# The second feed-forward part by seven block products, in two phases of 768 tokens

## What is computed

```
x += 0.5 * g1 * swiglu(modulate(rmsnorm(x), sh1, sc1), ffn1)
x += g2 * concat(window_attention, mla_attention) @ w_out
x += 0.5 * g3 * swiglu(modulate(rmsnorm(x), sh3, sc3), ffn2)
x  = rmsnorm(x)

def swiglu(h, wg, wu, wd):          # wg, wu: 1024 x 2816, wd: 2816 x 1024
    return (silu(h @ wg) * (h @ wu)) @ wd
```

## Time and profile before

| | |
|---|---|
| median of three runs | 3179.14 us |
| profiled execution, its own span | 3173.7 us |
| TensorE busy in it | 3075.7 us, 97% |
| VectorE, ScalarE, GpSimd busy | 1526.7, 956.5, 802.9 us |
| first matmul of the out-projection | 1928.30 us |
| matmuls in the span | 14129 |

### The profile page before, as it was taken

How to read it: one execution, slowest core, us unless ns; L and a number is a source line. 1 busy time by engine, 2 the same in 40 slices (tenths; PEclk the granted TensorE clock), 3 DMA queues, 4 the chain that set the end, 5 groups by cost and what they waited for, 6 DMA issues and landing times.

```text
span 3173.7 us, 40407 instructions
## 1 busy us (share of the span) xinstructions
PE 3075.7 (97%) x14129; PEld 2457.0 (77%) x14129; DVE 1526.7 (48%) x2651; ACT 956.5 (30%) x1669; POOL 802.9 (25%) x531
## 2 busy tenths in 40 slices
PE   7999999999999989997989999999999999999998
PEld 3888888888888868885656667788888888888887
DVE  5576667776671266886544331542322123231234
ACT  6311111111111146766767774331111111111112
POOL 0111111111111143334557665421111111111110
PEclk9999999999999999998999999999999999999999
DMA  7121212212121023557322244211110110101102
GB/s 267 39 69 57 62 52 79 68 58 64 48 74 34 27 95 124 144 146 168 99 59 75 78 105 130 84 43 34 33 33 26 40 32 27 33 26 40 33 27 87
DMA packets 282857, 223.60 MB, mean 70 GB/s; under 512 B 17179, under 2 KB 254094, under 8 KB 282766
## 3 DMA queue, kind: packets, MB, share of 16 engines
q1 hardware_dynamic: 282766, 222.41, 23.8%
...
## 4 chain that ended last, share of the span: by engine, by line
PE 43%; POOL 8%; issue 6%; DVE 3%; ACT 1%; SPq 1%; DMA 0%; DVEq 0%; POOLq 0%; ACTq 0%
PE PS L479 14%; PE PS L480 13%; PE PS L481 13%; POOL XT_r L1956 8%; PE PS L735 0%; PE PS L1655 0%; DVE XT L648 0%; DVE PS L634 0%; ACT z_sb L1173 0%; DVE y_sb L2221 0%; PE PS L1692 0%; DVE kT_st L1358 0%; SPq L2003 0%; DMA scr_kb<-kT_st 0%; ACT hid_hi L578 0%
## 5 line engine op out<-in xcount | busy, mean ns | idle before, releaser
L479 PE MATMUL PS<-H_hi,W_hi 128*128 128x512 f32 x2304 | 900.6, 391 | 1.4 <-DVE H_lo L1910 1.4
L480 PE MATMUL PS<-H_lo,W_hi 128*128 128x512 f32 x2304 | 897.0, 389 | 0.0
L481 PE MATMUL PS<-H_hi,W_lo 128*128 128x512 f32 x2304 | 896.9, 389 | 0.0
L473 POOL TENSOR_TENSOR W_lo<-raw,W_hi 128x1024 fp32r<-128x1024 f32 x132 | 317.2, 2409 | 1846.8 <-ACT W_hi L441 1846.8
L648 DVE SCALAR_TENSOR_TENSOR XT<-PS,mod,XT 128x512 f32<-128x512 f32 x528 | 395.1, 749 | 301.7 <-PE PS L481 301.5
L479 PEld LDWEIGHTS PS<-H_hi,W_hi 128*128 128x128 f32 x2304 | 432.9, 188 | 94.1 <-issue 2.5
L441 ACT ACTIVATE W_hi<-raw 128x1024 fp32r<-128x1024 f32 x132 | 137.3, 1056 | 1215.5 <-PE PS L481 1214.4
L480 PEld LDWEIGHTS PS<-H_lo,W_hi 128*128 128x128 f32 x2304 | 432.9, 188 | 90.6 <-issue 1.4
L481 PEld LDWEIGHTS PS<-H_hi,W_lo 128*128 128x128 f32 x2304 | 432.8, 188 | 89.8
L634 DVE TENSOR_TENSOR PS<-hid_g,PS 128x512 f32<-128x512 f32 x132 | 91.6, 694 | 763.2 <-PE PS L481 753.1
L479 PE MATMUL PS<-hid_hi,W_hi 128*128 128x512 f32 x1056 | 417.1, 395 | 4.2 <-DVE XT L648 2.7
...
## 6 DMA issues: line engine op xcount, KB each, us to landing
...
raw<-in_ffn_wg SPq DMA_DIRECT2D x44, 512.0 KB, 4.0
raw<-in_ffn_wu SPq DMA_DIRECT2D x44, 512.0 KB, 4.0
raw<-in_ffn_wd SPq DMA_DIRECT2D x44, 512.0 KB, 3.6
...
raw<-in_w_out SPq DMA_DIRECT2D x22, 512.0 KB, 3.6
...
```

What stands on the lines that cost most here:

```text
L473: pool.tensor_tensor(W_lo[:, n % WS, :], raw[:, n % RS, :], W_hi[:, n % WS, :].bitcast(F32), ALU.subtract).then_inc(w_ready, 1)
L479: pe.matmul(out, w_hi, m_hi, start=first, stop=False)
L480: pe.matmul(out, w_hi, m_lo, start=False, stop=False)
L481: return pe.matmul(out, w_lo, m_hi, start=False, stop=last)
```

## The change

The second feed-forward part is written anew, and the out-projection before it is cut in four chunks of 384 tokens in place of three of 512.

The block scheme: the 1024 input features are two halves, the 256 hidden columns of a round are two halves, and the 768 tokens of a phase are two halves of 384. Gate (or up) of a round is then a product of 2x2 blocks with 2x2 blocks, eight block products in the plain form. Here it is seven, with sums of weight blocks (A11, A12, A21 + A22 and so on, 7 weight units a round, gate in the left and up in the right half of a unit) and sums of activation blocks (B11, B21, T1 to T4, B22). A block product has 4 blocks of features by 3 matmuls, for gate and for up. Results are collected in four pairs of PSUM banks: ScalarE keeps copies of some (`part_keep_act`), VectorE adds them back (`st_add_dve`). Down stays plain: 16 steps of 6 matmuls with 384 columns, in eight banks in turn.

There are 22 rounds: phase 0 takes tokens 0 to 767 through 11 rounds, phase 1 the tokens 768 to 1535, so each weight is read and split twice. Weights come in quarters of 128x4x128 for gate and up (`quart`, four pairs a round), GpSimd makes the four weight sums (`st_sum`) and nine low splits a round. The activation operands of a phase are built once: `op_x_dve` normalises a block of 768 columns, `op_shift_act` adds the shift, `op_t_dve` makes a difference T of 4x384 columns, `op_hi_act` copies high, `op_lo_dve` makes the low part. For phase 0 that happens during the last chunk of the out-projection and behind it, for phase 1 in round 10 and the beginning of round 11.

The diff, cut to its core:

```
+NB = 384
+HT = 2 * NB
+NR = FT // 2
+NWC = TOK // NB
+UN = 9
+PN = 7
+B11, B21, T1, T2, T3, T4, B22 = range(PN)
...
         def wo_act(act):
-            for i in range(NCH * KD):
+            for i in range(NWC * KD):
                 if i >= RS:
                     wo_split_hi(act, i)
                 c, m = i // KD, i % KD
...
+                if c == NWC - 1:
+                    if m < 4:
+                        op_shift_act(act, 0, 2 * m)
+                        op_shift_act(act, 0, 2 * m + 1)
+                    else:
+                        for j in ((B11, B21), (T1,), (T2,), ())[m - 4]:
+                            op_hi_act(act, 0, j)
+            for j in (T3, T4, B22):
+                op_hi_act(act, 0, j)
...
         def wo_dve(dve):
-            for i in range(NCH * KD):
+            for i in range(NWC * KD):
...
+                gate_add(dve, i % WOB, 1, m, c, wo_added)
+                if c == NWC - 1:
+                    if m < 2:
+                        op_x_dve(dve, 0, 2 * m)
+                        op_x_dve(dve, 0, 2 * m + 1)
+                    elif m == 2:
+                        op_t_dve(dve, 0, T1)
+                        op_x_dve(dve, 0, 4)
+                        op_x_dve(dve, 0, 5)
...
+        def op_x_dve(dve, h, k):
+            if h == 0 and k == 0:
+                dve.wait_ge(wo_done, (NWC - 1) * KD)
+                dve.wait_ge(rstd_ready, 2 * NCH + 2)
+            if h == 1 and k == 0:
+                dve.wait_ge(st_steps, st_at(NR - 1, product_step(T3, 1)))
+                dve.wait_ge(rstd_ready, 2 * NCH + NWC)
+            if h == 1 and k == KD // 2:
+                dve.wait_ge(st_steps, st_at(NR - 1, product_step(B22, 1)))
+            row = SLf[:, KD * (k // 4) + 4 + k % 4, 0:2, :].rearrange("p c n -> p (c n)")
+            by = (rstd_a, rstd_b)[h][:, :, :].rearrange("p c n -> p (c n)")
+            for a, b, s, a0, b0 in phase_span(h):
+                mm = dve.scalar_tensor_tensor(out=row[:, a0:b0], in0=XT[:, k, a:b], scalar=hscale[:, 2, k, s:s + 1],
+                                              in1=by[:, a0:b0], op0=ALU.mult, op1=ALU.mult)
+            mm.then_inc(op_x, 1)
+        def op_shift_act(act, h, k):
+            act.wait_ge(op_x, OPX0 + h * XN + (k + 1 if k < KD // 2 else k + 2))
+            row = SLf[:, KD * (k // 4) + 4 + k % 4, 0:2, :].rearrange("p c n -> p (c n)")
+            for _, _, s, a0, b0 in phase_span(h):
+                mm = act.activation(row[:, a0:b0], row[:, a0:b0], ACT.Identity, bias=mod[:, SH3 * KD + k, s:s + 1])
+            mm.then_inc(op_shift, 1)
+        OP_T = {T1: (T3, B11), T2: (B22, T1), T4: (B21, T2), T3: (B22, T3)}
...
+        UNIT_FROM = (A11Q, A12Q, None, A11Q, A21Q, A22Q, A12Q)
...
+        def st_hi_act(act, R, u, nxt=0):
+            if u in (0, 1, 5):
+                act.wait_ge(quart_landed[UNIT_FROM[u]], R * 32 + (32 * nxt + 32 + QUART0))
+            elif u < PN:
+                act.wait_ge(sum_ready, R * 4 + (4 * nxt + {2: 1, 3: 3, 4: 2, 6: 4}[u]))
+            else:
+                act.wait_ge(down_landed[u - PN], R * 16 + (16 + DOWN0))
+            if is_round(R, 0) and u < 3 and not nxt:
+                act.wait_ge(wo_done, NWC * KD - 2 + u)
+            elif u < 3:
+                act.wait_ge(st_steps, st_at(R, SN * nxt - SN + (2 * PN if u == 0 else SN)))
+            else:
+                act.wait_ge(st_steps, st_at(R, 2 * (u - 3) + 2))
+            act.activation(W_hi[:, st_slot(u), :], unit_src(u), ACT.Copy).then_inc(unit_hi, 1)
...
+        def st_sum(pool, R, no, nxt=0):
+            out, a, b, op = ((qsum[:, :, :], quart[:, A21Q], quart[:, A22Q], ALU.add),
+                             (quart[:, A21Q], quart[:, A11Q], quart[:, A21Q], ALU.subtract),
+                             (quart[:, A11Q], qsum[:, :, :], quart[:, A11Q], ALU.subtract),
+                             (quart[:, A12Q], quart[:, A12Q], quart[:, A11Q], ALU.subtract))[no]
+            if no == 0:
+                if nxt:
+                    pool.wait_ge(unit_ready, unit_at(R, PN + 1))
+                for q in (A21Q, A22Q):
+                    pool.wait_ge(quart_landed[q], R * 32 + (32 * nxt + 32 + QUART0))
+            else:
+                pool.wait_ge(sum_ready, R * 4 + (4 * nxt + no))
+            if no >= 2:
+                pool.wait_ge(unit_ready, unit_at(R, UN * nxt + no - 1))
+            pool.tensor_tensor(flat(out), flat(a), flat(b), op).then_inc(sum_ready, 1)
+        def st_pool(pool):
+            def body(R, h):
+                for u in (1, 2):
+                    st_lo_pool(pool, R, u)
+                if is_round(R, 0):
+                    pair_up(pool, 2, NWC - 1)
+                st_sum(pool, R, 3)
+                for u in range(3, UN):
+                    st_lo_pool(pool, R, u)
+                if not is_round(R, 2 * NR - 1):
+                    st_next_pool(pool, R, 1)
+            def st_next_pool(pool, R, nxt):
+                st_sum(pool, R, 0, nxt)
+                st_lo_pool(pool, R, 0, nxt)
+                st_sum(pool, R, 1, nxt)
+                st_sum(pool, R, 2, nxt)
+            st_next_pool(pool, 0, 0)
+            st_rounds(pool, body)
+        PRODUCT_BANK = (BX, BY, BZ, BX, BX, BX, BZ)
+        DOWN_BANKS = (6, 7, 0, 1, 2, 3, 4, 5)
...
+        def st_act(act):
+            def body(R, h):
+                st_hi_act(act, R, 1)
+                st_hi_act(act, R, 2)
+                if is_round(R, NR):
+                    for j in (T1, T2, T3, T4, B22):
+                        op_hi_act(act, 1, j)
+                part_keep_act(act, R, 0)
+                part_keep_act(act, R, 1)
+                st_hi_act(act, R, 3)
+                if is_round(R, 0):
+                    sums_act(act, 2, NWC - 1, (0, 4))
+                st_hi_act(act, R, 4)
+                st_silu_act(act, R, 0)
+                st_hid_act(act, R, 0)
+                if is_round(R, 0):
+                    sums_act(act, 2, NWC - 1, (4, KD))
+                st_hi_act(act, R, 5)
+                if is_round(R, 0):
+                    root_act(act, 2, NWC - 1)
+                part_keep_act(act, R, 2)
+                part_keep_act(act, R, 3)
+                st_hi_act(act, R, 6)
+                part_keep_act(act, R, 4)
+                part_keep_act(act, R, 5)
+                st_hi_act(act, R, 7)
+                st_silu_act(act, R, 1)
+                st_hid_act(act, R, 1)
+                st_silu_act(act, R, 2)
+                st_hi_act(act, R, 8)
+                st_hid_act(act, R, 2)
+                if is_round(R, NR - 1):
+                    for k in range(4):
+                        op_shift_act(act, 1, k)
+                st_silu_act(act, R, 3)
+                st_hid_act(act, R, 3)
+                if is_round(R, NR - 1):
+                    op_hi_act(act, 1, B11)
+                    for k in range(4, KD):
+                        op_shift_act(act, 1, k)
+                    op_hi_act(act, 1, B21)
+                if not is_round(R, 2 * NR - 1):
+                    st_hi_act(act, R, 0, 1)
+            st_hi_act(act, 0, 0)
+            st_rounds(act, body)
...
+        def st_product(pe, R, h, j):
+            for role in range(2):
+                if role == 0:
+                    pe.wait_ge(unit_ready, unit_at(R, j + 1))
+                    if is_round(R, h * NR):
+                        pe.wait_ge(op_ready, OPR0 + h * PN + j + 1)
+                if j in PRODUCT_OPENS and not is_round(R, 0):
+                    n = PRODUCT_BANK[j] + role
+                    pe.wait_ge(st_hid, hidden_at(R, {BX: 3, BY: 1, BZ: 4}[PRODUCT_BANK[j]] - 4, HID0))
+                    pe.wait_ge(st_acc, acc_at(R, n + 11 - 2 * KD))
+                if j in (T2, T3, T4):
+                    pe.wait_ge(part_kept, R * 6 + ({T2: 1, T3: 3, T4: 5}[j] + role))
+                if j == B22:
+                    pe.wait_ge(part_added, R * 5 + (2 + role))
+                out = PS[:, PRODUCT_BANK[j] + role, 0:NB]
+                for kp in range(4):
+                    w = slice(role * CH + kp * P, role * CH + (kp + 1) * P)
+                    w_hi, w_lo = W_hi[:, st_slot(j), w], W_lo[:, st_slot(j), w]
+                    m_hi, m_lo = operand(SL, X4, j, 0, kp), operand(SL, X4, j, 1, kp)
+                    pe.matmul(out, w_hi, m_hi, start=j in PRODUCT_OPENS and kp == 0, stop=False, skip_group_check=True)
+                    pe.matmul(out, w_hi, m_lo, start=False, stop=False, skip_group_check=True)
+                    mm = pe.matmul(out, w_lo, m_hi, start=False, stop=kp == 3, skip_group_check=True)
+                mm.then_inc(st_steps, 1)
+        def st_down(pe, R, h):
+            ends = is_round(R, 2 * NR - 1)
+            for t in range(2):
+                pe.wait_ge(unit_ready, unit_at(R, PN + 1 + t))
+            for i in range(2 * KD):
+                c, m = i // KD, i % KD
+                if i == 0:
+                    pe.wait_ge(st_hid, hidden_at(R, 3, HID0))
+                if i == 6:
```

(12 more changed lines are left out.)

386 lines of the change are left out of this document (290 added, 96 removed).

## The result

The changed kernel takes 3205.6 us (median of four, 3205.23 to 3207.44) beside 3179.4: a ratio of 1.0083 (95% interval 1.0069 to 1.0097). It is slower by 26 us, as forecast (3210, range 3176 to 3238). Its profiled execution spans 3203.9 us.

The account below looks back on a forecast made before the run. TensorE's matmuls were taken as the bound. 3173.7 - 75.2 + 34.0 + 15.9 + 10.7 + 30.0 + 14 + 1 (last round and tail) = 3204.1, with 5.4 around the span 3209.5: 3210 us, range 3176 to 3238.

Parts of the forecast that it names:

- Parts 1 and 2: Matmul work saves 75.2 us; steady rounds last 45.75 us and cost nothing extra, with 0.26 us of slack.
- rival (c): Steady rounds: the 0.26 us slack is missing, adding 11 to 22 us, 3221 to 3232; chance 0.17.
- rival (d): Matmuls of 384 columns: the weight load binds at 188 ns each, +97 us, 3307; chance 0.02.
- part 1: Matmul work: -75.2 us by measured rows; the page's formula gave -81.7 for the feed-forward and was not used.
- Part 3: Out-projection's last chunk: weight copies held back behind bias additions on ScalarE make TensorE wait 34.0 us.
- Rival (a): Out-projection's last chunk: weights are copied far enough ahead, 34 us of waits and 5 of clock vanish, 3171; chance 0.09.
- Part 4: Out-projection to first product: a wait of 11.9 to 12.1 us plus 3.8 for VectorE-GpSimd collisions, 15.9.
- Part 5: Round 0: second product waits 2.9 us, two sums of squares take 2.6, T2 waits 5.2; sum 10.7.
- Part 6: Phase switch: waits of 3.5, 7.7 (ScalarE's unit 0 copy), 8 (B21), 10.5 (T2); 30.0 us with roundings, 14 collision.
- Part 7: Clock falls to 1.2 GHz behind long waits: 1.2 to 1.4 us lost on each of ten, 14 us.
- Around the span: Whole kernel: median 3179.14 us against a profiled span of 3173.7; the 5.4 us between were kept in the forecast.
- Rival (b): VectorE and GpSimd hardly collide: parts 4 and 6 lose 3.8 and 14 us, 3192, or 3178 without clock loss; chance 0.14.

Follow-up runs that it names:

- e7: Changed kernel with the high copy of weight unit 1 done in 16 pieces in 18 rounds: 1.0144 of the kernel before, 19 us more than the changed kernel.
- e1: Changed kernel with ScalarE's weight copies in the out-projection's last chunk one unit ahead: 0.9985 of the kernel before, 31 us less than the changed kernel.
- e8: Changed kernel with ScalarE's weight copies in the out-projection's last chunk two units ahead: 0.9975 of the kernel before, 34 us less than the changed kernel.
- e4: Changed kernel with round 11's unit 0 copy ahead of the operand copies and three operand copies moved back: 1.0076 of the kernel before.
- e2: Changed kernel with unused matmuls filling five waits of the out-projection's last chunk: 1.0044 of the kernel before, 12 us less than the changed kernel.
- e9: Changed kernel with out-projection copies two units ahead, the first product's weights prepared earlier, and GpSimd's splits ahead of sums: 3159.4 us, 0.9944 of the kernel before.

## Why the prediction was right

The sign, the mechanism and the places of the large waits were right, and 3210 was 4 us too high. By its terms:

- **Parts 1 and 2**: right. The period is 45.76 us (45.75 forecast), and the play is 0.1 to 0.2 us by e7 (0.26), thinner than I had it but never used up. The period alone rules out rival (c), which I had given 0.17, and with it rival (d), the weight load. The formula that I set beside part 1 is called that of the isolated gap in the section that I named of the Trainium skill ("TensorE: Matmul & The Clock Gate", Back-to-back issue gap), not that of a stream; the sum did not use it.
- **Part 3**: 32.5 us of waits for 34.0. Rival (a) said that the copies would stand far enough ahead; the rows show them held back, and e1 and e8, which move them alone, take most of the waits away. So the order is the cause of these waits. What is left behind it is GpSimd's order and its turns with VectorE.
- **Part 4**: 14.05 for 15.9. The collisions were 1.2 us on T2's low part and 1.2 on GpSimd's split, 2.4 and not 3.8; the other 11.7 us are the 11.9 to 12.1 of the sum.
- **Part 5**: 4.8 us of waits and two sums for 10.7. B21 waited 0.44 and not 2.9: the first product, at the low clock, took 6.67 us in place of 4.16 and so covered the weight sums. A clock loss and a wait behind it are not simply added. With the sums, some 2.6 us, it is 7.4 for 10.7.
- **Part 6**: 20.0 for 30.0, the term most wrong. B21 waited 4.9 in place of 8 and T2 4.8 in place of 10.5. The prediction prints no working for the 8, but three pairs at 1.75 + 2.39, less a first product of 4.16, are 8.3. Measured were three GpSimd operations in 11.5 us, less a first product that took 6.57 at the low clock: 4.9. So most of the miss is that of part 5 once more, the clock loss counted beside a wait that it shortens. This is read from the timeline and was not run by itself, and why T2's 10.5 was twice too large stays open. The 7.7 was measured as 7.56, but its stated cause, the place of ScalarE's copy, was not the whole of it: e4 moved the copy, that wait fell to 2.5, and waits of 7.5 us at the down steps and at B21 took its place (4.9 before).
- **Part 7**: 26 us for 14. Behind each of the eleven waits of 2.8 us or more the clock was low for 3.4 to 5.6 us, 1.7 to 2.8 us lost each, where I had scaled from the loss of 1.4 behind the short wait of the earlier trace rows. e2 priced it at 2.4 each. That short wait was itself a poor measure: in the changed kernel it is again 1.41 us, at 1930.00, with nothing altered ahead of it, and 5.7 us at the lower level follow, 2.8 lost; in e9 3.0 us follow the same wait.
- **Around the span**: I had left 5.4 us there. In every run on record that has both numbers, of the kernel before too, the time is 1.7 to 1.9 us above the span. So the 5.4 were not around the span: the profiled execution before was some 3.6 us faster than the median. In the other direction 1.7 us of the difference of the spans lie ahead of the out-projection, in front of anything that changed in work.

In sum: waits 17 us too high, clock 12 too low, and 3.6 too much around the span. These misses have opposite signs, and that the total came within 4 us is in part luck. Put together with the loss at 1930 and the 1.7 us ahead of it, the measured terms leave 1 to 2 us that I can't place. Rival (b), few collisions, had the right tendency for parts 4 and 6, which came to 34 us where I had 46 and (b) would have 28, and the wrong one for the clock.
